# Part of the modulation products of a two-block transformer kernel summed over rows by VectorE, from pieces loaded on GpSimd's queue

## The reference

```
silu_c = jax.nn.silu(c)
silu_cc = jax.nn.silu(c_ctx)
for l in range(DEPTH):
    m_lat = (silu_c @ w_mod[l] + b_mod[l]).reshape(Bsz, N_MOD, 1, D)     # N_MOD 9, D 1024
    m_ctx = (silu_cc @ w_mod[l] + b_mod[l]).reshape(N_MOD, D)
    x = x + 0.5 * m_lat[:, 2] * swiglu(modulate(rms_norm(x), m_lat[:, 0], m_lat[:, 1]), ffn_in[l, 0], ffn_out[l, 0])
    ctx = ctx + 0.5 * m_ctx[2] * swiglu(modulate(rms_norm(ctx), m_ctx[0], m_ctx[1]), ffn_in[l, 0], ffn_out[l, 0])
    ...   # the mixer of the layer: l = 0 attention beside an rwkv scan, l = 1 windowed attention
    x = x + 0.5 * m_lat[:, 8] * swiglu(modulate(rms_norm(x), m_lat[:, 6], m_lat[:, 7]), ffn_in[l, 1], ffn_out[l, 1])
...
def swiglu(h, w_in, w_out):
    gate, up = jnp.split(h @ w_in, 2, axis=-1)
    return (jax.nn.silu(gate) * up) @ w_out
```

## Time and profile before

| what | us |
|---|---|
| median of 3 runs | 3808.41 (3801.29 to 3816.84) |
| profiled execution, span | 3809.4 |
| PE busy | 3587.4 (94%) |
| DVE busy | 1836.3 (48%) |
| ACT busy | 1418.9 (37%) |
| POOL busy | 60.0 (2%) |

### The profile page before, as it was taken

How to read it: one execution, slowest core, us unless ns; L and a number is a source line. 1 busy time by engine, 2 the same in 40 slices (tenths; PEclk the granted TensorE clock), 3 DMA queues, 4 the chain that set the end, 5 groups by cost and what they waited for, 6 DMA issues and landing times.

```text
span 3809.4 us, 62156 instructions
## 1 busy us (share of the span) xinstructions
PE 3587.4 (94%) x27294; PEld 2960.9 (78%) x27294; DVE 1836.3 (48%) x3143; ACT 1418.9 (37%) x2303; POOL 60.0 (2%) x98
## 2 busy tenths in 40 slices
PE   6999999888889999999987999999999989999898
PEld 4777885677668888877874998777887768879898
DVE  2223445666654233423265553654464443566575
ACT  3123334434334222323244543443243332445553
POOL 0000000000010000000000000020000000010000
PEclk8999999999999999999998999999999999999999
DMA  5454123222243233243225552121324552223463
GB/s 194 163 183 134 59 83 127 102 102 102 102 77 110 91 99 100 90 142 122 89 89 212 174 180 96 58 78 56 100 83 172 177 173 93 89 91 127 145 190 113
DMA packets 257918, 453.93 MB, mean 119 GB/s; under 512 B 14096, under 2 KB 157584, under 8 KB 243184
## 3 DMA queue, kind: packets, MB, share of 16 engines
q1 hardware_dynamic: 253840, 441.68, 34.6%
q0 software_dynamic: 3808, 8.27, 1.3%
HBM read 447.24 MB, written 1.94 MB: 118 GB/s over the span
## 4 chain that ended last, share of the span: by engine, by line
PE 81%; DVE 10%; ACT 4%; DMA 3%; issue 1%; SPq 0%; DVEq 0%; ACTq 0%
PE bank L1072 80%; DVE W L1859 2%; DVE W L1868 2%; DVE WR L1859 2%; DMA ring<-in_w_mod 1%; ACT WR L1524 1%; ACT W L1524 1%; PE bank L1295 1%; DMA ring<-in_w_up 1%; DVE H L1859 1%; DVE HL L1859 1%; DMA ring<-in_w_ada 1%; DVE X L1868 0%; ACT H L1524 0%; DVE small L2136 0%
## 5 line engine op out<-in xcount | busy, mean ns | idle before, releaser
L1072 PE MATMUL bank<-HH,WR 128*128 128x512 f32 (+1 forms) x9312 | 2430.9, 347 | 74.9 <-DVE WR L1859 42.0
L1072 PEld LDWEIGHTS bank<-HH,WR 128*128 128x128 f32 x9312 | 1643.3, 192 | 334.3 <-DVE WR L1859 54.4
L1072 PE MATMUL bank<-HL,WR 128*128 128x512 f32 (+1 forms) x4656 | 1601.3, 344 | 0.0
L1859 DVE TENSOR_TENSOR WR<-ring,WR 128x2048 fp32r<-128x2048 f32 (+3 forms) x300 | 673.8, 2250 | 859.9 <-ACT WR L1524 859.4
L1524 ACT ACTIVATE WR<-ring 128x2048 fp32r<-128x2048 f32 (+3 forms) x300 | 562.6, 1881 | 1200.1 <-PE bank L1072 819.5
L1072 PEld LDWEIGHTS bank<-HL,WR 128*128 128x128 f32 x4656 | 895.4, 192 | 96.9
L1524 ACT ACTIVATE W<-bank 64x256 f32<-64x256 f32 (+4 forms) x662 | 285.8, 442 | 388.6 <-PE bank L1072 342.1
L1072 PE MATMUL bank<-W 64*64 64x64 f32 (+5 forms) x6304 | 351.7, 247 | 41.4 <-ACT W L1524 20.5
L1072 PEld LDWEIGHTS bank<-W 64*64 64x64 f32 (+3 forms) x6304 | 266.1, 140 | 131.6 <-issue 47.2
L1868 DVE SCALAR_TENSOR_TENSOR W<-bank,vec,W 128x510 f32<-128x510 f32 (+1 forms) x206 | 130.6, 634 | 190.2 <-ACT W L1524 186.6
L1524 ACT ACTIVATE W<-bank,small 128x512 f32<-128x512 f32 (+2 forms) x183 | 113.1, 622 | 225.8 <-DVE small L2136 154.1
(11 more groups left out here) (111 smaller groups left out, 2022.0 us busy)
## 6 DMA issues: line engine op xcount, KB each, us to landing
ring<-in_ffn_in SPq DMA_DIRECT2D x176, 512.0 KB, 5.0
ring<-in_w_mod SPq DMA_DIRECT2D x72, 1024.0 KB, 5.4
ring<-in_w_in SPq DMA_DIRECT2D x52, 1024.0 KB, 5.1
ring<-in_w_ada SPq DMA_DIRECT2D x48, 1024.0 KB, 6.5
ring<-in_ffn_out SPq DMA_DIRECT2D x176, 256.0 KB, 3.6
ring<-in_w_up SPq DMA_DIRECT2D x88, 512.0 KB, 5.0
ring<-in_w_down SPq DMA_DIRECT2D x88, 256.0 KB, 3.6
ring<-in_even_w_in SPq DMA_DIRECT2D x8, 1024.0 KB, 5.1
```

What stands on the lines that cost most here:

```text
L1072: return e.matmul(o, l, r, start=start, stop=stop, skip_group_check=True)
L1859: put(e.tensor_tensor(o, a, b, op), *events)
```

## The change

17 of the 30 blocks of 1024 columns (m0: 2 to 8, m1: 0 to 5, a0: 0 to 3) leave the path above. For such a block (`row_sums`) GpSimd's queue loads eight pieces of 128x1024 (512 KB, step `rows_in`) into the two halves of one ring slot, which is taken from the weights for the length of the job (`rows_begin`, `rows_end`), so that the weights go through the other two. DVE multiplies piece k by the silu's value for each row and adds it to an accumulator, one for each of the two vectors (step `rows`, `W<-ring,vec,W`). PE then sums over the 128 rows by four matmuls with ones (`rows_sum`), ScalarE copies, PE turns the sums (`rows_tr`) and DVE adds the bias. A piece k is loaded into the half that piece k-2 has left.

Five blocks are summed in ffn_in and one in ffn_out of each of f00, job 2 and f10 (the block m1 5 for one vector only, the silu of c, since layer 1 writes no context back). In ffn_in the rate is 0.55 pieces for each m, in ffn_out 0.9 for each m, so that the eight pieces of that block come with deep slab 0 and the first step of deep slab 1. What a block leaves for PE after its last piece stands in PENDING and is taken by the next job's first group. 68 of the 120 quads go; there are 12 left in the rwkv stage, 8 in the odd attention and none in f00, the lora stage and f10. The silu of both conditions is made once at the start. The hold of a "bcast" bank is 8 takes, not 6.

```diff
+        def rows_begin():
+            i = hold["keep"] = (hold["slot"] + 1) % NS
+            hold["halves"] = [IN_SLOT[i], IN_SLOT[i]]
+        def rows_end():
+            hold["slot"], hold["keep"], hold["halves"] = hold["keep"], None, None
...
+        def row_sums(jobs, buf):
+            tail = []
+            for t, idx, nv in jobs:
+                for k in range(KD):
+                    s = rows_slab(TABLES[t][0], k, idx)
+                    ORDER.append(("rows_in", s))
+                    ORDER.append(("rows", t, idx, k, s, nv, buf))
+                    if tail and k in (2, 4):
+                        ORDER.append(tail.pop(0))
+                    yield
+                tail = [("rows_sum", t, idx, s, nv, buf), ("rows_tr", t, idx, nv)]
+                buf = 1 - buf
+            PENDING.extend(tail)
...
-            lin_deep(name + "o", w_out, G, ntok, mod, i0 + 2, after, name + "i")
+            if rows:
+                for _ in rows[0]:
+                    pass
+                now(PENDING)
+            lin_deep(name + "o", w_out, G, ntok, mod, i0 + 2, after, name + "i",
+                     each=background(rows[2], rows[3]) if rows else None)
...
-        ffn("f00", A["ffn_in"][0, 0], A["ffn_out"][0, 0], 0, NT, 0, "ne", (itertools.islice(cols["m0"], 18), 0.85))
+        ffn("f00", A["ffn_in"][0, 0], A["ffn_out"][0, 0], 0, NT, 0, "ne",
+            rows=(row_sums(pairs_of("m0", 2, 7), 0), 0.55, row_sums(pairs_of("m0", 7, 8), 0), 0.9))
...
-        ffn("2", A["ffn_in"][0, 1], A["ffn_out"][0, 1], 6, NT, 0, "nf10", (skewed(), 0.2))
-        ffn("f10", A["ffn_in"][1, 0], A["ffn_out"][1, 0], 0, NT, 1, "no", (itertools.islice(cols["a0"], 9), 0.5))
+        ffn("2", A["ffn_in"][0, 1], A["ffn_out"][0, 1], 6, NT, 0, "nf10", (skewed(), 0.2),
+            rows=(row_sums(pairs_of("m0", 8, 9) + pairs_of("m1", 0, 4), 0), 0.55, row_sums(pairs_of("m1", 4, 5), 0), 0.9))
+        ffn("f10", A["ffn_in"][1, 0], A["ffn_out"][1, 0], 0, NT, 1, "no",
+            rows=(row_sums(pairs_of("m1", 5, 6, 1) + pairs_of("a0", 0, 3), 1), 0.55, row_sums(pairs_of("a0", 3, 4), 0), 0.9))
...
-                    if any(use[r] >= i for r in befores(todo[0], "raw")):
+                    if any(use[r] >= i for r in befores(todo[0], "raw", "rows")):
                         break
...
+            def rows(t, idx, k, s, nv, buf):
...
+                for v in range(nv):
...
+                    if k == 0:
+                        ts(ACC[buf][v], rows_of(s), c, None, ALU.mult, None, *events)
+                    else:
+                        q.wait_ge(DVES, ("rows", t, idx, k - 1, v))
+                        stt(ACC[buf][v], rows_of(s), c, ACC[buf][v], ALU.mult, ALU.add, *events)
...
+            def rows_in(s):
...
+                    q.wait_ge(DVES, ("rows", x["before"]))
+                e.dma_start(rows_of(s), x["parts"][0]).then_inc(ROWS[x["half"]].sem, ROWS[x["half"]].mark(("raw", s), by=16))
```

More of the change, by code:

```diff
@@ L241, in program @@
         SLABS = []
-        hold = {"split": 0, "slots": 3, "slot": -1, "keep": None}
+        hold = {"split": 0, "slots": 3, "slot": -1, "keep": None, "halves": None}
         IN_SLOT = [None] * NS
@@ L268, in slab, with rows_slab, rows_of @@
             return IN_SLOT[i]
+        def rows_begin():
[3 more added lines that the diff above has]
+            hold["slot"], hold["keep"], hold["halves"] = hold["keep"], None, None
+        def rows_slab(w, k, idx):
+            i, h = hold["keep"], k % 2
+            SLABS.append(dict(parts=[w[P * k:P * k + P, 1024 * idx:1024 * idx + 1024]], kc=1, w=1024, kind="rows", half=h,
+                              split_from=hold["split"], slots=hold["slots"], ring=i, before=hold["halves"][h],
+                              n=sum(x["kind"] == "split" for x in SLABS)))
+            IN_SLOT[i] = hold["halves"][h] = len(SLABS) - 1
+            return IN_SLOT[i]
         def slot(s):
             return ring[SLABS[s]["ring"]]
+        def rows_of(s):
+            h = SLABS[s]["half"]
+            return slot(s).rearrange("p k c -> p (k c)")[:, 1024 * h:1024 * h + 1024]
         def landed(s):
@@ L1014, in program @@
                 use[step[6]] = i
+            if step[0] == "rows":
+                use[step[4]] = i
             if step[0] == "lora_done":
                 use[LORA["s"]] = i
-        befores = lambda s, kind: [x["before"] for x in SLABS[:s + 1] if x["before"] is not None and SLABS[x["before"]]["kind"] == kind]
+        befores = lambda s, *kinds: [x["before"] for x in SLABS[:s + 1] if x["before"] is not None and SLABS[x["before"]]["kind"] in kinds]
         steps, at_hold, behind_ = [], 0, []
         for i, step in enumerate(ORDER):
-            if step[0] in ("slab", "slab_h", "slab_k", "mod_mm"):
+            if step[0] in ("slab", "slab_h", "slab_k", "mod_mm", "rows"):
                 steps += [("rest", s) for s in behind_]
@@ L1026, in program @@
                 assert not todo or todo[0] not in befores(step[6], "split")
+            if step[0] == "rows":
+                assert not todo or todo[0] not in befores(step[4], "split")
             n = None
@@ L1057, in take @@
                 at[0] += 1
-                n = next(i for i, (t, b) in enumerate(shut_) if not (holder[b] and holder[b][0] == "bcast" and at[0] - t < 6))
+                n = next(i for i, (t, b) in enumerate(shut_) if not (holder[b] and holder[b][0] == "bcast" and at[0] - t < 8))
                 b = shut_.pop(n)[1]
@@ L1193, in mod_tr, with rows_sum, rows_tr @@
                            C("sel", 0, 2 * nb, 0, 32 * nb), True, True)
+                x.then_inc(MM.sem, MM.mark(key))
+                shut(key)
+            def rows_sum(t, idx, s, nv, buf):
+                key = ("rows", t, idx)
+                o = take(key)
+                q.wait_ge(IN["first"], ("in", "first"))
+                q.wait_ge(DVES, ("rows", s))
+                for j in range(2):
+                    for v in range(nv):
+                        i = 32 * (nv * j + v)
+                        x = mm(o[i:i + 32, :], C("ones", 0, 32), ACC[buf][v][:, 512 * j:512 * j + 512], True, True)
+                x.then_inc(MM.sem, MM.mark(key))
+                shut(key)
+            def rows_tr(t, idx, nv):
+                key = ("rowsc", t, idx)
+                n = 2 * nv
+                q.wait_ge(ACTS, ("mrow", t, "rows", idx))
+                o = take(key)
+                for m in range(4):
+                    x = mm(o[:, n * m:n * m + n], RROW[0:32 * n, m * P:(m + 1) * P], C("sel", 0, 2 * n, 0, 32 * n)[:, ::2], True, True)
                 x.then_inc(MM.sem, MM.mark(key))
```

111 lines of the change are left out of this document (90 added, 21 removed).

## The result

The changed kernel takes 3825.18 us (median of 8 runs, 3821.9 to 3827.74) against 3811.04 (8 runs, 3801.23 to 3818.58): ratio 1.0037, 95% interval 1.0024 to 1.005. It is 14 us slower, clear of its interval, and within the 0.5% that the prediction called "the same"; the forecast was 3830, the range 3790 to 3868. The profiled execution of after has a span of 3822.7 us, 13.3 more than before.

What follows compares the result with a forecast made beforehand. The prediction took TensorE (PE), holding 81% of the span, as the bound, with room on DVE and the DMA engines. Its terms summed to +21.4 us on the profiled execution's 3809.4: forecast 3830, range 3790 to 3868.

Steps and rivals of the forecast that it cites:

- f00, ffn_in: First feed-forward job: 16 quads leave and six blocks come, 25.2 us before against 12.1 after, -13.
- The deep stall: Start of ffn_out in three jobs: lo split of deep slab 1 stands behind pieces k0 to k4, +39.6 us (27 to 50).
- The skew collision: Job 2's ffn_in: 16 skew DMAs on GpSimd's queue delay piece k3 and the split of slab i9, +21.7 us (8 to 31).
- Job 2 without its stalls: Job 2, which had no modulation work, gets the same six blocks as f00: +12.1 us.
- The lora stage: Lora stage: 12 quads holding 18.97 us of PE leave, half counted as gain, -9 us (-3 to -14).
- The rwkv stage: Rwkv stage: 24 of 36 quads leave, and most waits for w_mod with them, -25 us (-8 to -38).
- Odd attention: Odd attention: 8 of 16 quads leave, where PE also waits 7.3 us for w_ada, -9 us (-3 to -14).
- DVE late in ffn_in: In ffn_in: DVE's work fits a slab with some 2.5 us spare, late where pieces fall unevenly, +2 us (0 to 15).
- Rival B: Lo split of deep slab 1 is in time, deep and most skew stalls go: 3768, or 3785 with 6 us left each; chance 0.13.
- Rival D: Every piece lands late, sharing DMA engines with weights, from f = 7 us; ffn_in slabs stretch, about 3865 us; chance 0.06.
- Rival E: Rwkv stage loses clock without the quads, 2.7 us in each of eight chunks, giving back 22 us: 3852 us; chance 0.06.
- Rival C: Gains and stalls cancel, stalls at their lower ends (27 + 8): 3809 us; chance 0.25.

Runs made afterwards that it cites:

- both edits: Changed kernel with the 16 skew DMAs moved to job 11 and splits no longer waiting for pieces on GpSimd's queue: 3766.97 us, ratio 0.9875.
- e2: Changed kernel with one planner rule changed, so a split no longer waits for pieces on GpSimd's queue: 3789.65 us, ratio 0.9937.
- e1: Changed kernel with the 16 skew DMAs moved out of job 2 to the start of job 11: 3801.83 us, ratio 0.9974.
- e6: Kernel with both edits, its 12 quads of the rwkv stage moved back into the lora stage: 3748.11 us, ratio 0.985.
- e9: Kernel of e6 with one of eight PSUM banks held through the rwkv stage, nothing done in it: 3755.72 us.

## Why the prediction was right

**The start** (forecast +3): +3.03. **f00, ffn_in** (25.2 before without the 2.7 of clock, 9.9 after, so -12.6): -13.1. Quads in line, blocks in line and the fifth block at the passage cost what the rows had said.

**The deep stall** (forecast 3 x 13.2 = 39.6): up to the start of deep slab 2, after loses 11.5, 11.7 and 11.6 us in the three jobs to the kernel with both edits, 34.8 together. The mechanism and the place were right; the term was 5 too large, because f was 3.75 to 4.2, in the lower half of its range, so that the waits were 9.1 to 10.0 and not 10.5, and the clock cost 2.3, 2.2 and 1.5 us where 2.7 had been charged each time. One reason in it was wrong: the prediction has the split behind the pieces "since its ring slot is given by a piece". The slot isn't; with e2's rule the same split is made at 298.19, ahead of all pieces of the block, and nothing but the planner's rule had held it back. On the price of a DMA from GpSimd's queue, an estimate of 3.2 us by the Trainium skill ("DMA: Bandwidth & Descriptors", section "Anatomy of one DMA — SWDGE (gpsimd) path") stands against 3.75 in the chain and a median of 4.7 over the 104 pieces of w_mod; none of the 136 pieces landed in under 3.7, and the row of before (3.6) was nearer.

**The skew collision** (forecast 21.7): 24.4, taken from the kernel without it (22.57 of wait, the rest clock). The queue was held 36.9 us, not 30.9: the sixteenth DMA waited 24.13 and not 18.18 beside the pieces.

**Job 2 without its stalls** (+12.1) came to 46.0 - 24.4 - 11.7 = 9.9; **f10** as a whole to +11.0 of 12.2 forecast, so -0.6 without its stall where -1 was forecast.

**The lora stage** (forecast -9): -4.1, and with the 2.2 of f00's sixth block, which stands in that stretch, -6.3. That it is a gain at all is partly luck: with the same instructions the stage of e1 took 254.7 us, 4.9 more than before. **The rwkv stage** (-25): -26.7. **Odd attention** (-9): -12.0. The shares of the busy time had been taken at a half and six tenths with little to hold them. Of the three together -43 was forecast and -45.0 came, the 2.2 set aside: the errors of single stages, up to 3 us, nearly cancelled, and no run here shows that the shares themselves were right.

**DVE late in ffn_in** (+2): nothing. The four waits shown are all that PE has of over 2 us in the three jobs past their first slabs.

**The sum.** At the last matmul after stands at +12.1 where +21.4 was forecast. Of the 9.3 less, the deep stall makes 4.8, odd attention 3.0, job 2's blocks 2.2, DVE in ffn_in 2.0 and the rwkv stage 1.7; the skew collision and the lora stage went the other way by 2.7 each, and 1.0 is spread over the rest.

Rival B needed the split in time, which it was not. Rival D needed landings of 7 us; their median was 4.7. Rival E, the clock, was aimed at the wrong stage: the granted clock of the rwkv stage fell from 0.98 to 0.95 (700 to 1060 us), the edge of what the prediction had set for E, but the stage gave back 26.7 us and not the 3 that E left of it; the lora stage lost more clock (below). Rival C, gains and stalls cancelling within half a percent, is near to what happened in size; its way is not: it had both stalls at their lower ends (27 and 8), and they took 34.8 and 24.4. And by the prediction's own line at 3827 us the result belongs to "the same", which had 0.36, and not to "slower", which had 0.52: right in mechanism and range, it put too much weight on the side beyond half a percent. (The count in the prediction, 17 of 30 blocks, is right; the "20 of 36" that it is set against stands nowhere in this text.)

## What to carry to other kernels

Moving work to an idle engine pays here only where what is urgent on that engine doesn't end up behind it: compare the order on that engine and on each DMA queue, and follow the chain of buffers (sum, issue, landing) that stands ahead of the urgent step. A planner's rule that was written for one queue should not be applied to transfers of another; two edits of a line or two turned a loss of 14 us into a gain of 44. Small DMAs that cost nothing on an idle queue stop being free when something with a deadline shares the queue.

## What the runs showed of the hardware

**The lora stage's clock differs from run to run of the same instructions.** After and the kernel with the skew moved have the same instructions in the same order up to job 2's ffn_in, but their lora stages took 245.7 and 254.7 us. The windows of PE in 620 to 660 us, before, after, with the skew moved, and with the quads of e6:

```profile
620.00:660.00 40.00, 37.93 (x220) 16.24 (x220) 22.95 (x60) 21.80 (x49) 0.00 (x0) 0.94 0.56 201
```

```profile
620.00:660.00 40.00, 34.30 (x156) 16.59 (x155) 22.68 (x59) 21.37 (x51) 0.00 (x0) 0.78 0.00 1
```

```profile
620.00:660.00 40.00, 39.09 (x123) 17.82 (x122) 18.14 (x46) 17.17 (x41) 0.00 (x0) 0.50 0.00 0
```

```profile
620.00:660.00 40.00, 37.94 (x232) 16.30 (x230) 24.94 (x66) 22.71 (x54) 0.00 (x0) 1.00 0.57 207
```

PE appears busier at 0.50 than at 0.94, with fewer matmuls: busy time alone hides it, the clock's column shows it. With 12 quads in the stretch the granted clock was 0.94 (before) and 1.00 (e6); without them 0.78 and 0.50. So 12 quads, 13 us of PE work, kept more of the clock. With quads or fillers the stage took 247.9 to 249.8 us in five executions, without them 245.7 to 254.7 in seven: they made it steadier, and on average no longer. The Trainium skill ("TensorE: Matmul & The Clock Gate", section "What's actually happening") has the gate follow how busy the engine has recently been; the windows agree in that the level fell when work was taken out, but why the same instructions got 0.78 once and 0.50 once stays open.

**A PSUM bank less in a stage of many short products cost 7.7 us of 362**, with no work in it (e9, one profiled execution).

**Sixteen DMAs of 54 KB in rows of 31 floats held GpSimd's queue 31 to 39 us** (before, after, e1), and the issue of the sixteenth alone waited 18.2 to 25.1; what it waits for the profile doesn't show. Nothing on PE shows it until something behind them is needed.
